# From the RWKV mixer to the mixture of experts, turned to token rows before the norm

## The chip, the cores and the metric

The kernel runs on one core of a Trainium2 chip. The metric is the device time of one launch in microseconds (us); a median over several runs is compared. The trace counts its times from the first instruction of the profiled execution.

## The reference

Two layers of a hybrid trunk on one sequence of 256 tokens of width 1024 (and 256 context tokens). Layer 0 is a Hyena mixer and a dense SwiGLU, layer 1 an RWKV-7 mixer and a mixture of eight experts. What matters here is the middle of layer 1:

```python
hx = layer_norm(ALPHA * hx + g1x * (y @ rw_w_out), ln_g[1, 0], ln_b[1, 0])
h = hx * (1.0 + sc2x) + sh2x
logits = h @ router                                # (256, 8)
top_val, top_idx = top_k(logits, 2)                # softmax over the two
fx = sum(combine[:, e] * ((silu(h @ w1[e]) * (h @ w3[e])) @ w2[e]) for e in range(8))
hx = layer_norm(ALPHA * hx + g2x * fx, ln_g[1, 1], ln_b[1, 1])
```

Everything is float32. An expert has 3 x 1024 x 3584 weights, and all eight are read in each launch.

## The kernel before

The program is written by hand, engine by engine, with semaphores. A tile called `arena` holds all of SBUF, and every stage lays its own names over it. In layer 1 the activations are kept channel-major: `XT[:, k, :]` holds channel tile k (of KT = 8, 128 channels each), with tokens along the row.

**RWKV.** Eight head pairs follow one another (`pair(i, more)`, L1464 on TensorE, L2276 on ScalarE, L2549 on POOL, L3038 on VectorE); the last has `more=False` and nothing ahead to prepare. Its gaps on TensorE are filled with the output product `YT @ rw_w_out`: `out_products` (L1455) takes the first seven of eight channel tiles of YT. The order of the eight output tiles is `OUT_ORDER`. `pair_done` (L3167) is raised by VectorE when YT is complete. Before that the SP queue has loaded each pair's weights (L861 to L892), and, once the last pair's gate product is done (L894), it loads the kept residual into XT, the router weights, the order table and the eight tiles `WO[k]` of rw_w_out, one after another (L896 to L903).

**The handover.** TensorE waits for `pair_done`, raises `expert_products` (L1686), and adds the last channel tile to the eight output sums (L1697). VectorE forms the residual of each tile (L3183), TensorE the mean (L1691), VectorE centres (L3190), ScalarE squares (L2371), TensorE forms the variance (L1704), ScalarE takes Ln and Exp (L2066, L2067), VectorE scales (L3196). ScalarE makes the modulated activation `UT` (L2379), and TensorE makes the logits as 8 rows (L1715), turns them and UT to token rows (L1719, L1725), and later XT scaled by POOL (L2593) for the residual y (L1732). The gate row of layer 1 is spread to all partitions by a product with a diagonal (POOL L2588, TensorE L1709, ScalarE L2376). ScalarE copies the turned rows to `UTOK` and `XTOK` (L2385, L2392).

**Choice and ranking, on VectorE.** Top two of eight (L3204 to L3216), a count of each token's place in its expert's list on TensorE (L1741 to L1745), the slot numbers (L3226, L3228), and `choose` (L3232), which makes the one-hot selection `pick` of the first expert; `first_expert` is raised. TensorE then gathers that expert's tokens (`gather`, L1751), and ScalarE and VectorE split the result in a high and a low part (L2397, L3237). Meanwhile VectorE ranks the experts by load (L3271 to L3289); POOL computes the combination shares (L2600 to L2605). `routed` counts these steps.

**Experts.** `large` and `small` alternate, four times: a large expert in 128 slots with split float32r products (`hidden_products` L1778, `down_products` L1809), a small one in 64 slots with plain float32 (L1863, L1897). Weights come through a ring of `ERN` = 8 slots of 1.5 to 2 MB, which ScalarE rounds to a high part (L2420) and VectorE to a low part (`low_digits`, L3247). On the SP queue each load (L919) waits for the step of `expert_products` that frees its slot; in the first round the slots that lie below `sq_at` are loaded at once, the others after `ln_scaled` 24 (L929). In the first large expert VectorE does a small yield (L3307), the first low digit, xg_low (L3237), three low digits, four additions to XTOK (L3301), then the up digits.

```python
for n, m in enumerate(OUT_ORDER):
    if n >= 4:
        mean3(n - 4)
    mm(out_sum(m), WO[KT - 1][:, m * P:(m + 1) * P], YT[:, KT - 1, :], start=False, stop=True,
       skip_group_check=True).then_inc(sem("out_full"), 1)
```

## Time and profile before

| | |
|---|---|
| median of 3 runs | 2230.41 us (2229.41 to 2232.9) |
| span of the profiled execution | 2236.2 us, 56085 instructions |
| granted TensorE clock over the span | 0.987 |
| TensorE busy | 2143.9 us (96%) |
| VectorE, ScalarE, POOL busy | 1177.1, 913.5, 179.7 us |
| DMA | 491.19 MB, mean 220 GB/s |
| last output tiles of the mixer to the first expert product | 1318.6 to 1354.6 us |

The profiled execution has no time of its own beside its span. Of the whole, the Hyena layer and its dense part take the first 780 us, RWKV the time to 1320, the experts the rest. A line of the profile names the engine and the line of the kernel (L1778), the operation, what it writes and reads, and a count; an entry "idle before <-" names what ended the idle time of the engine before it. PE is TensorE, PEld its weight load, DVE VectorE, ACT ScalarE, POOL GpSimd, and a q behind a name is an engine's instruction queue (SPq issues the DMAs).

### The profile page before, as it was taken

What the parts mean: (1) busy time and instruction counts of PE and PEld (TensorE: products, weight loads), DVE (VectorE), ACT (ScalarE), POOL (GpSimd) and SP (SyncE); (2) the same over time, 40 slices, a digit from 0 to 9 for tenths busy, and PEclk for the clock granted to TensorE, in tenths of its full rate; (3) what the DMA queues carried; (4) which work ended last, traced back from release to release, by engine and by line L of the source; (5) the groups of instructions that cost most, each with busy time, mean ns of one, the idle gap of its engine ahead of it and who ended that gap; (6) DMA issues with size and microseconds to landing.
All of it is one profiled execution on the core that took longest, in us unless ns stands there. A gap on an engine that the chain in (4) does not pass through costs nothing.

```text
span 2236.2 us, 56085 instructions
## 1 busy us (share of the span) xinstructions
PE 2143.9 (96%) x24686; PEld 1587.3 (71%) x24686; DVE 1177.1 (53%) x1581; ACT 913.5 (41%) x1196; POOL 179.7 (8%) x181
## 2 busy tenths in 40 slices
PE   8999999899999989999999899999999899989997
PEld 4577667688888747888888778953895399449843
DVE  3544595522233386666666539830982198129812
ACT  3422013522222185555555327720771177027600
POOL 2100272100000002200000100000000000000000
PEclk9999999999999999999999999999999999999999
DMA  8466406333322341111110258999999999999996
GB/s 292 153 225 235 160 1 184 118 94 94 95 94 101 99 153 35 35 35 35 35 35 26 80 202 317 366 363 407 406 407 398 407 407 407 403 406 407 407 405 259
DMA packets 220597, 491.19 MB, mean 220 GB/s; under 512 B 14631, under 2 KB 107711, under 8 KB 220095
## 3 DMA queue, kind: packets, MB, share of 16 engines
q1 hardware_dynamic: 218974, 482.44, 58.0%
q10 hardware_dynamic: 1442, 6.06, 0.8%
q8 instruction: 148, 2.42, 0.4%
q14 instruction: 33, 0.27, 0.0%
HBM read 486.37 MB, written 2.10 MB: 218 GB/s over the span
## 4 chain that ended last, share of the span: by engine, by line
PE 80%; DVE 5%; DMA 5%; SPq 4%; ACT 3%; issue 2%; POOL 0%; ACTq 0%; DVEq 0%
PE bank L1778 13%; PE bank L1809 7%; PE bank L1863 5%; SPq L919 4%; DMA expert_w<-in_moe_w_dram 4%; PE bank L1245 4%; PE bank L1246 4%; PE bank L1247 4%; PE bank L1151 2%; PE bank L1413 2%; PE bank L1122 2%; PE bank L1124 2%; PE bank L1123 2%; PE bank L1377 2%; PE bank L1262 2%
## 5 line engine op out<-in xcount | busy, mean ns | idle before, releaser
L3247 DVE TENSOR_TENSOR w_low<-expert_w,w_high 128x1792 fp32r<-128x1792 f32 (+1 forms) x192 | 383.8, 2023 | 43.2 <-ACT w_high L2420 41.5
L2420 ACT CAST w_high<-expert_w 128x1792 fp32r<-128x1792 f32 (+1 forms) x192 | 324.8, 1699 | 106.2 <-PE bank L1778 71.3
L1863 PE MATMUL bank<-expert_w,arena 128*64 128x448 f32 x1024 | 199.1, 541 | 1.5 <-DMA expert_w<-in_moe_w_dram 1.3
L1863 PEld LDWEIGHTS bank<-expert_w,arena 128*64 128x64 f32 x1024 | 72.3, 137 | 117.8 <-issue 116.7
L1778 PE MATMUL bank<-w_high,xg_high 128*128 128x448 f32 x512 | 147.0, 368 | 8.0 <-DVE xg_low L3237 7.7
L1778 PE MATMUL bank<-w_high,xg_low 128*128 128x448 f32 x512 | 145.1, 365 | 0.0
L1778 PE MATMUL bank<-w_low,xg_high 128*128 128x448 f32 x512 | 145.0, 364 | 0.0
L1245 PE MATMUL bank<-u_high,ring_high 128*128 128x512 f32 x352 | 138.7, 394 | 2.0 <-DVE u_low L2888 1.9
L1246 PE MATMUL bank<-u_low,ring_high 128*128 128x512 f32 x352 | 137.9, 392 | 0.0
L1247 PE MATMUL bank<-u_high,ring_low 128*128 128x512 f32 x352 | 137.6, 391 | 0.0
L2467 ACT ACTIVATE arena<-bank 128x448 f32<-128x448 f32 x16 | 8.7, 545 | 259.8 <-PE bank L1863 259.8
L1897 PE MATMUL bank<-expert_w,arena 128*64 128x512 f32 x448 | 101.6, 602 | 9.6 <-issue 8.9
L1778 PEld LDWEIGHTS bank<-w_high,xg_high 128*128 128x128 f32 x512 | 95.7, 190 | 19.2 <-DVE xg_low L3237 11.4
L1778 PEld LDWEIGHTS bank<-w_low,xg_high 128*128 128x128 f32 x512 | 97.0, 189 | 6.7
L1778 PEld LDWEIGHTS bank<-w_high,xg_low 128*128 128x128 f32 x512 | 96.8, 189 | 6.6
L3368 DVE TENSOR_TENSOR arena<-arena,bank 128x448 f32<-128x448 f32 x16 | 9.9, 621 | 158.1 <-PE bank L1863 158.1
L1809 PE MATMUL bank<-w_high,hid_high 128*128 128x512 f32 x224 | 88.0, 393 | 0.0
L1809 PE MATMUL bank<-w_high,hid_low 128*128 128x512 f32 x224 | 87.3, 390 | 0.0
L1809 PE MATMUL bank<-w_low,hid_high 128*128 128x512 f32 x224 | 87.2, 389 | 0.0
L1897 PEld LDWEIGHTS bank<-expert_w,arena 128*64 128x64 f32 x448 | 33.1, 138 | 72.5 <-issue 72.0
L2907 DVE TENSOR_TENSOR arena<-arena,bank 128x512 f32 (+1 forms) x22 | 15.1, 688 | 125.1 <-ACT arena L2157 125.1
L1245 PEld LDWEIGHTS bank<-u_high,ring_high 128*128 128x128 f32 x352 | 66.5, 189 | 16.9 <-issue 2.9
(454 smaller groups left out, 4208.6 us busy)
## 6 DMA issues: line engine op xcount, KB each, us to landing
expert_w<-in_moe_w_dram SPq DMA_DIRECT2D x128, 1792.0 KB, 18.6
expert_w<-in_moe_w_dram SPq DMA_DIRECT2D x32, 2048.0 KB, 19.3
arena<-in_mod_w_dram SPq DMA_DIRECT2D x48, 1024.0 KB, 8.6
expert_w<-in_moe_w_dram SPq DMA_DIRECT2D x32, 1536.0 KB, 18.9
arena<-in_ffn_w_dram SPq DMA_DIRECT2D x44, 512.0 KB, 5.0
arena<-in_hy_w_in_dram SPq DMA_DIRECT2D x12, 1024.0 KB, 5.3
arena<-in_rw_w_rkv_dram SPq DMA_DIRECT2D x48, 256.0 KB, 2.9
arena<-in_ffn_w_dram SPq DMA_DIRECT2D x11, 1024.0 KB, 4.8
```

The costliest lines, as they stand in the source:

```text
L919: sp.dma_start(dst, src).then_inc(expert_landed(s)[0], 16)
L1122: pe.matmul(bank[m % 4][:, :], wh[:, k, :], uh, start=(k == 0), stop=False)
L1123: pe.matmul(bank[m % 4][:, :], wh[:, k, :], ul, start=False, stop=False)
L1245: pe.matmul(bank[b + h][:, :], wh[:, c, :], uh, start=(k == 0), stop=False)
L1246: pe.matmul(bank[b + h][:, :], wh[:, c, :], ul, start=False, stop=False)
L1247: last = pe.matmul(bank[b + h][:, :], wl[:, c, :], uh, start=False, stop=(k == KT - 1))
L1778: last = pe.matmul(bank[b0 + v][:, 0:EH], x[:, k, :], w_[:, kk, v * EH:v * EH + EH], start=(k == 0 and x is XGH and w_ is wh), stop=(k == ...
L1809: last = pe.matmul(bank[4 + i_][:, :], x[:, f, :], w_[:, f - 4 * half, :], start=(c == 0 and f == 0 and x is HTH and w_ is wh), stop=(c == ...
L1863: last = pe.matmul(b[hd(v), 0:EH], small_x[:, k, :], w[:, kk, v * EH:v * EH + EH], start=(k == 0), stop=(k == KT - 1))
L1897: last = pe.matmul(bank[4][hd(v), :], small_hid[:, f, :], w[:, g, 512 * v:512 * v + 512], start=(c == 0 and f == 0), stop=(c == EC - 1 and ...
L2420: act.copy(high_piece(kind, n), piece(kind, ering[q % ERN], n // 2, n % 2))\
L3247: dve.tensor_tensor(piece(kind, low[s], n // 2, n % 2), piece(kind, ering[s], n // 2, n % 2), high_piece(kind, n).bitcast(F32), ALU.subtract)\
```

## The change

The handover is done by token. The residual tiles, now in `X3` (KT x 256), are turned to token rows directly behind the output product, in PSUM banks 0, 1, 4 and 5. VectorE takes mean and variance of each token by bn_stats, ScalarE one square root. The logits are made from the raw residual with router weights that hold the norm's gain and the modulation (`router_u`), and are corrected per token by the mean, the reciprocal deviation and two sums over the router's rows (`sum_row`). The normalised rows (`XTOK`) come from ScalarE, in four halves (`z_tok`). u is made of them with two rows of gain and shift, for tokens 0 to 127 on POOL, for tokens 128 to 255 on VectorE; y = ALPHA x (gain, shift) on POOL. The gain, shift and gate rows are stored to DRAM as three rows during pair 5's loads on SP and loaded again to all partitions. The loads of the residual and of the first four WO tiles follow the last pair's key product, and the router loads stand before the first pair. `expert_products` is raised before the last pair, the early slots are those below `x_at`, and the others wait for `out_full` 24. `OUT_ORDER` goes.

```diff
+        rows_kept = nc.dram_tensor("rows_kept", (3, D), F32, kind="Internal").ap()
...
-        low_k = 3
+        low_k = 4
+        WO = [arena[:, x_at + k * D:x_at + (k + 1) * D] for k in range(KT)]
+        u_gain, u_shift = (arena[:, x_at + 2 * KT * T + D * i:x_at + 2 * KT * T + D * i + D] for i in range(2))
...
-        early_slots = [s for s in range(ERN) if slot_at[s] + slot_words[s] <= sq_at]
+        early_slots = [s for s in range(ERN) if slot_at[s] + slot_words[s] <= x_at]
...
+            load("ld_router", rt_w, a["moe_router"][0].rearrange("(k p) e -> p k e", p=P))
+            load("ld_router", order_table, consts[4])
...
+                if i == KT - 3:
+                    sp.wait_ge(sem("rows_ready"), 1)
+                    for r, cols_ in enumerate((mod_g, mod_b, modv[1][:, 5 * KT:6 * KT, 0])):
+                        load("rows_kept", rows_kept[r].rearrange("(k p) -> p k", p=P), cols_)
...
-            step(sp, "ahead_products", "gate", KT - 1)
+            step(sp, "ahead_products", "keys", KT - 1)
             sp.wait_ge(sem("ld_tail"), 16)
             for k in range(0, KT, 2):
-                load("ld_tail", XT[:, k:k + 2, seg[1]], residual_kept[:, k:k + 2, :])
+                load("ld_tail", X3[:, k:k + 2, :], residual_kept[:, k:k + 2, :])
                 sp.wait_ge(sem("ld_tail"), 16 + 8 * (k + 2))
-            load("ld_tail", rt_w, a["moe_router"][0].rearrange("(k p) e -> p k e", p=P))
-            load("ld_tail", order_table, consts[4])
-            for k in range(KT):
-                load("ld_out", WO[k], a["rw_w_out"][k * P:(k + 1) * P, :])
-                sp.wait_ge(sem("ld_out"), 16 * (k + 1))
+            for name, row in (("ln_g", y_gain), ("ln_b", y_shift)):
+                load("ld_y_rows", row, a[name][1, 0:1, :].partition_broadcast(P))
+            sp.wait_ge(sem("rows_kept"), 48)
+            load("ld_row_gate", rowG, rows_kept[2:3, :].partition_broadcast(P))
+            for k in range(low_k):
+                load_wo(k)
+            step(sp, "ahead_products", "gate", KT - 1)
+            for k in range(low_k, KT):
+                load_wo(k)
+            for r, row in enumerate((u_gain, u_shift)):
+                load("ld_u_rows", row, rows_kept[r:r + 1, :].partition_broadcast(P))
             sp.wait_ge(sem("pair_done"), 2)
...
-                        sp.wait_ge(sem("ln_scaled"), 24)
+                        sp.wait_ge(sem("out_full"), 24)
...
+            pe.sem_inc(sem("expert_products"), len(STEPS["expert_products"]))
             pair(KT - 1, False)
+            pe.wait_ge(sem("rows_ready"), 1)
+            mm(bank[0][:, 0:2 * N_EXP], ones, router_sum, start=True, stop=True).then_inc(sem("sums_full"), 1)
             pe.wait_ge(sem("pair_done"), 2)
-            pe.sem_inc(sem("expert_products"), len(STEPS["expert_products"]))
             pe.wait_ge(sem("ld_out"), 16 * KT)
...
+            def turn_tile(m):
+                if m == 0:
+                    pe.wait_ge(sem("sums_taken"), 1)
+                pe.wait_ge(sem("residual_done"), 16 + m + 1)
+                for tt in range(2):
+                    last = pe.transpose(tok_bank(tt, m // 4)[:, m % 4 * P:m % 4 * P + P], X3[:, m, tt * P:tt * P + P], ident)
+                last.then_inc(sem("tile_turned"), 1)
+            def tile_logits(m):
+                for tt in range(2):
+                    last = mm(bank[2][:, tt * N_EXP:(tt + 1) * N_EXP], X3[:, m, tt * P:tt * P + P], router_u[:, m, :],
+                              start=(m == 0 and tt == 0), stop=(m == KT - 1), skip_group_check=True)
+                return last
+            for m in range(KT):
                 mm(out_sum(m), WO[KT - 1][:, m * P:(m + 1) * P], YT[:, KT - 1, :], start=False, stop=True,
                    skip_group_check=True).then_inc(sem("out_full"), 1)
+                if m >= 3:
+                    turn_tile(m - 3)
+            turn_tile(5)
+            tile_logits(0)
+            turn_tile(6)
+            tile_logits(1)
+            turn_tile(7)
+            for m in range(2, KT):
+                last = tile_logits(m)
             last.then_inc(sem("logits_full"), 1)
...
             pe.wait_ge(sem("first_expert"), 1)
+            pe.wait_ge(sem("u_tok"), 4)
             gather(0).then_inc(sem("first_expert"), 1)
...
+            act.activation(eps[:, 4:5], eps[:, 0:1], ACT.Sqrt)
+            act.wait_ge(sem("tok_var"), 1)
+            act.activation(stat[:, :, 2:3], whole[:, :, 1:2], ACT.Sqrt, bias=eps[:, 0:1]).then_inc(sem("tok_std"), 1)
+            for tt in range(2):
+                act.wait_ge(sem("tok_shift"), tt + 1)
+                for half in range(2):
+                    act.activation(XTOK[:, tt, half * 512:half * 512 + 512], tok_bank(tt, half)[:, :], ACT.Identity,
+                                   bias=stat[:, tt, 0:1], scale=stat[:, tt, 3:4]).then_inc(sem("z_tok"), 1)
+            act.wait_ge(sem("routed"), 2)
+            act.activation(w12[:, :, 1:2], w12[:, :, 0:1], ACT.Exp).then_inc(sem("w_exp"), 1)
+            act.wait_ge(sem("u_tok"), 4)
...
+                        act.wait_ge(sem("y_tok"), 2)
...
+            pool.wait_ge(sem("ld_y_rows"), 32)
+            for row in (y_gain, y_shift):
+                row_step(pool.tensor_scalar(row, row, float(ALPHA), 0.0, ALU.mult, ALU.add))
+            pool.wait_ge(sem("ld_u_rows"), 32)
+            for half in range(2):
+                cs = slice(half * 512, half * 512 + 512)
+                pool.wait_ge(sem("z_tok"), half + 1)
+                row_step(pool.tensor_tensor(UTOK[:, 0, cs], XTOK[:, 0, cs], u_gain[:, cs], ALU.mult))
+                pool.tensor_tensor(UTOK[:, 0, cs], UTOK[:, 0, cs], u_shift[:, cs], ALU.add).then_inc(sem("u_tok"), 1)
+            pool.wait_ge(sem("z_tok"), 4)
+            for tt in range(2):
+                row_step(pool.tensor_tensor(XTOK[:, tt, :], XTOK[:, tt, :], y_gain, ALU.mult))
+                pool.tensor_tensor(XTOK[:, tt, :], XTOK[:, tt, :], y_shift, ALU.add).then_inc(sem("y_tok"), 1)
...
             for i in range(KT - 1):
                 pair(i, True)
+                if i == 1:
+                    fold_router()
             pair(KT - 1, False)
...
+            for half in range(2):
+                dve.wait_ge(sem("tile_turned"), 4 * half + 4)
+                for tt in range(2):
+                    last = dve.bn_stats(out=halves[:, tt, 6 * half:6 * half + 6], in_=tok_bank(tt, half)[:, :])
+            link(last)
+            for tt in range(2):
+                last = dve.bn_aggr(out=whole[:, tt, :], in_=halves[:, tt, :])
+            last.then_inc(sem("tok_var"), 1)
...
+            dve.tensor_scalar(stat[:, :, 1:2], whole[:, :, 0:1], -1.0, None, ALU.mult)
+            centred_times_gain(0)
+            dve.wait_ge(sem("tok_std"), 1)
+            link(dve.reciprocal(stat[:, :, 3:4], stat[:, :, 2:3]))
+            dve.tensor_tensor(stat[:, :, 0:1], stat[:, :, 1:2], stat[:, :, 3:4], ALU.mult).then_inc(sem("tok_shift"), 1)
+            centred_times_gain(1).then_inc(sem("tok_shift"), 1)
...
             dve.wait_ge(sem("logits_full"), 1)
+            for tt in range(2):
+                last = dve.scalar_tensor_tensor(out=logit[:, tt, :], in0=sum_row[:, 0:N_EXP], scalar=stat[:, tt, 1:2],
+                                                in1=bank[2][:, tt * N_EXP:(tt + 1) * N_EXP], op0=ALU.mult, op1=ALU.add)
+            link(last)
+            for tt in range(2):
+                last = dve.scalar_tensor_tensor(out=logit[:, tt, :], in0=logit[:, tt, :], scalar=stat[:, tt, 3:4],
+                                                in1=sum_row[:, N_EXP:2 * N_EXP], op0=ALU.mult, op1=ALU.add)
...
             dve.sem_inc(sem("routed"), 1)
+            scaled_plus_shift(0)
             dve.wait_ge(sem("places_full"), 1)
...
             choose(0, slot_no).then_inc(sem("first_expert"), 1)
+            scaled_plus_shift(1)
+            dve.tensor_tensor(w12[:, :, 0:1], mx[:, :, 1:2], mx[:, :, 0:1], ALU.subtract).then_inc(sem("routed"), 1)
...
+            dve.wait_ge(sem("w_exp"), 1)
+            link(dve.tensor_scalar(w12[:, :, 0:1], w12[:, :, 1:2], 1.0, None, ALU.add))
+            link(dve.reciprocal(w12[:, :, 2:3], w12[:, :, 0:1]))
+            link(dve.tensor_tensor(w12[:, :, 3:4], w12[:, :, 2:3], w12[:, :, 1:2], ALU.mult))
...
+                        dve.wait_ge(sem("y_tok"), 2)
                         added((6, 7, 2, 3))
```

`centred_times_gain` takes the mean from a turned half in PSUM and multiplies by u_gain, `scaled_plus_shift` multiplies by the reciprocal deviation and adds u_shift, both for tokens 128 to 255. `fold_router` makes mod_g, mod_b, router_u and router_sum in seven small instructions.

## Rows read from the trace of the kernel before

**Rows 1.** Stretches: length, busy by engine, POOL last; granted clock, DMA share, GB/s.

```profile
1320.00:1350.00 30.00, 25.61 (x139) 18.22 (x137) 14.76 (x53) 17.11 (x29) 6.32 (x13) 0.94 1.03 407
1350.00:1360.00 10.00, 7.40 (x35) 5.86 (x36) 9.92 (x8) 7.59 (x7) 0.34 (x3) 1.00 0.29 115
1360.00:1480.00 120.00, 119.82 (x607) 106.44 (x607) 100.69 (x70) 81.59 (x64) 0.00 (x0) 1.00 0.95 352
1490.00:2190.00 700.00, 680.02 (x3488) 456.71 (x3486) 351.92 (x268) 297.69 (x294) 0.00 (x0) 0.99 1.03 405
```

**Rows 2.** SP queue's waits, 1240 to 1620 us: total, times, longest.

```profile
SPq L929 <- DVE arena L3196: 7.0, 1, 7.0
SPq L919 <- PEq L1686: 6.2, 1, 6.2
```

**Rows 3.** TensorE's timeline, 1318 to 1355 us: start, length, engine, line.

```profile
1318.58 0.59 PE L1697 MATMUL bank<-arena 128*128 128x256 f32 x2
...
1345.84 3.81 PE L1751 MATMUL bank<-arena 128*128 128x128 f32 x32 [0.23 <-DVE arena L3232]
...
1354.59 0.67 PE L1778 MATMUL bank<-w_high,xg_high 128*128 128x448 f32 x2 [1.37 <-DVE xg_low L3237]
```

**Rows 4.** VectorE's timeline, 1323 to 1364 us.

```profile
1323.96 0.48 DVE L3183 SCALAR_TENSOR_TENSOR arena<-bank,arena 128x256 f32<-128x256 f32 x1 [0.38 <-PE bank L1697]
...
1341.42 0.17 DVE L3202 COPY arena<-bank 128x16 f32<-128x16 f32 x1 [0.83 <-PE bank L1725]
...
1345.21 0.48 DVE L3232 TENSOR_SCALAR arena<-arena 128x128 f32<-128x128 f32 x2
...
1348.61 0.17 DVE L3289 TENSOR_TENSOR arena<-arena 128x16 f32<-128x16 f32 x1
...
1353.17 1.29 DVE L3237 TENSOR_TENSOR xg_low<-bank,xg_high 128x512 fp32r<-128x512 f32 x2
...
1362.57 2.02 DVE L3247 TENSOR_TENSOR w_low<-expert_w,w_high 128x1792 fp32r<-128x1792 f32 x1
```

**Rows 5.** Lines L3385 and L3391 (min/median/max ns), and ScalarE's timeline at 1343 us.

```profile
L3385 DVE BATCH_NORM_STATS2 arena<-bank x4: 681/687/698, 2224.1 to 2229.2; 128x6 f32<-128x512 f32 x4
...
L3391 DVE SCALAR_TENSOR_TENSOR arena<-bank,arena x4: 743/747/752, 2225.7 to 2230.8; 128x512 f32<-128x512 f32 x4
...
1343.74 1.07 ACT L2392 ACTIVATE arena<-bank 128x512 f32<-128x512 f32 x2
```

**Rows 6.** POOL's and VectorE's timelines around 891, 69, 286 and 1278 us, and line L2678.

```profile
890.82 0.68 DVE L2992 TENSOR_TENSOR arena<-arena 128x512 f32<-128x512 f32 x1
...
891.59 1.27 POOL L2532 TENSOR_TENSOR arena<-arena 128x512 f32<-128x512 f32 x1 [14.05 <-DVE arena L2992]
892.82 1.71 POOL L2532 TENSOR_TENSOR arena<-arena 128x512 f32<-128x512 f32 x1
...
892.14 1.27 DVE L2996 TENSOR_TENSOR arena<-arena 128x512 f32<-128x512 f32 x1
...
69.76 1.25 POOL L2495 TENSOR_TENSOR arena<-arena 128x512 f32<-128x512 f32 x1
...
L2678 DVE TENSOR_SCALAR arena<-arena x3: 174/174/649, 70.4 to 254.0; 128x16 f32<-128x16 f32 x3
...
286.75 1.75 DVE L2842 TENSOR_TENSOR arena<-arena 128x512 f32<-128x512 f32 x1
...
1278.76 1.90 POOL L2588 TENSOR_TENSOR arena<-arena 128x1024 f32<-128x1024 f32 x1
```

**Rows 7.** Two microseconds between two experts, columns as in rows 1.

```profile
1568.00:1570.00 2.00, 1.29 (x4) 0.01 (x1) 1.97 (x2) 2.00 (x3) 0.00 (x0) 0.56 1.04 406
```

**Rows 8.** Key weights of pair 6: SP's issue, ScalarE's first use; VectorE behind pair 1.

```profile
1096.15 3.20 SPq L871 DMA_DIRECT2D arena<-in_rw_w_rkv_dram  x2
...
1128.45 1.05 ACT L2218 CAST keys_w_high<-arena 128x1024 fp32r<-128x1024 f32 x1
...
966.57 0.45 DVE L3046 COPY_PREDICATED arena<-arena,bank 128x256 f32<-128x256 int32 x1 [1.92 <-PE bank L1472]
```

183 lines of the change are left out of this document (57 added, 126 removed).

## Prediction

> **What bounds the kernel now.** I read the stretches of time first. From 1490 to 2190 us the DMA queues move 405 GB/s: the expert weights set the pace there. At the handover they do not: they run full from 1320 to 1350, fall to 115 GB/s in the next ten microseconds and come to 352 in the first large expert, to 1480, in which TensorE is busy 119.82 of 120 us [rows 1]. The ring of eight slots is full, and a load starts when TensorE frees a slot. So what the change is worth is read at one place: how much earlier TensorE gets through the first large expert. Every later load follows from those slots, and the tail moves by the same amount.
>
> The SP queue's waits come second: 6.2 us for PE's queue at L1686, past the pair's end, and 7.0 us for the scaled tiles of L3196 [rows 2]. Then TensorE's timeline: the last output tiles start at 1318.58, the gather for the first expert at 1345.84 and its first gate product at 1354.59 [rows 3]. Between them stands a chain of norm, router, ranking and choice. Its last part runs on VectorE: the choice ends at 1345.69, the ranking at 1348.78, and then come the small yield, a low digit and xg_low, which ends at 1354.46 [rows 4]. VectorE is still the late one in the first gate: its first up digit ends at 1364.59, when TensorE is ready for it [rows 4]. Hence the measure is VectorE's chain: **each microsecond by which xg_low moves is a microsecond of the kernel**, up to the 23 us of queue that are unused there (10 x 292/407 and 120 x 55/407).
>
> **What goes and comes before the choice.** The output tiles still end about 1320.5, one small product (sums) later, at most 0.4 us by a tile of L1697 [rows 3]. Eight residuals of 0.48 us follow as before and end at 1324.2 [rows 4]; the transposes ride between the tiles, so the last ends near 1325.4. New on VectorE: four bn_stats of 0.69 (two before that moment, two after), two aggregations, the first product of 0.75, reciprocal and shift 0.4, the second 0.75 [rows 5], small ones at 0.2: 1329.1. ScalarE's root falls beside the first product, and its table is loaded long before. The router products left behind the last transpose are 24 instructions, at the gather's rate (32 in 3.81 [rows 3]) 2.9: 1328.3, hidden. Two pairs of logit instructions, 0.4 each as the small ones of rows 4 have it, and then from the copied logits to the choice 3.6 (3.79 less the copy) and 0.48 as now [rows 4]: the choice would be made at **1334.0** instead of 1345.7, 11.7 earlier. What it takes out is the mean, variance, Ln, Exp, eight scalings, the 8-row logits and half of 32 transposes.
>
> **What comes behind the choice.** One shifted product (0.7) and the weights' four small steps (0.7) now stand in the chain: 1.4 back. Unhindered, xg_low would come 10.3 to 10.5 us earlier.
>
> **Who shares the way.** The change puts eight POOL instructions exactly there: four of 128x512 for u from the first z half (1329.0: the shift at 1328.4 and one ScalarE half of 0.54 [rows 5]) and four of 128x1024 for y. POOL's multiply of 128x512 takes 1.27 us alone; 128x1024 took 1.90 once, with broadcast inputs, and twice 1.27 is 2.54 [rows 6]. I take 2.4, nearer to the same kind. So POOL is busy from 1329.0 to 1334.4 with u and to about 1344.7 with y.
> And such an instruction holds VectorE up. One of two SBUF inputs, 128x512, took 1.27 instead of 0.68 when it began 0.55 into POOL's: it ended 0.6 after POOL's end, and the next POOL instruction then took 1.71. A tensor_scalar of 16 elements took 649 ns against 174, until POOL's end; and when two VectorE instructions stood back to back, POOL went between them and the second took 1.75 [rows 6]. The two take turns, whole instructions at a time.
> The Trainium skill says so too (SBUF — State Buffer, Who interferes with whom): a VectorE instruction with two SBUF inputs contends with a GpSimd instruction that reads SBUF, the port pair is locked for a whole instruction, and tensor_scalar can fall under it as well. By that rule the sum is the one below, against this change; by a mere slowing of both it would be near the 10.4. The trace agrees with the lock [rows 6].
>
> **The sum under turns.** Before the choice VectorE has nine instructions of this kind: the second logit pair, two is_equal, two for the chosen, one shifted product, two for the pick. POOL has eight. Each waits for about one POOL instruction, so the choice comes when POOL ends, 1344.7 and not 1334.0. After it VectorE is free: 0.7 for the second half of u, 3.1 for the ranking (1345.69 to 1348.78 [rows 4]), 0.7 for the weights: 1349.2 against 1348.78, **0.4 us later**. If the short tensor_scalars did not wait, five stand before the choice, the four y instructions catch the second half, the subtraction, "above" and "moves", and the chain ends 1.2 earlier. With y at 1.90 all is 2.0 earlier, with 2.54 0.6 later. I take 0.4 us of gain, between the two readings; this case's own range is 3.2 of gain to 3.0 of loss (0.4, 0.6 and 2 for a slow gather, see next). The gather then starts at 1345.5 as now and needs 3.8 [rows 3]. The granted clock fell to 0.56, towards its 1.2 GHz level, after a pause of TensorE between experts [rows 7]; as it now pauses before the gather, that may take 2 to 4 us more, of which the yield and the low digit on VectorE cover 2. The wait for y before the four additions comes to nothing: VectorE gets there at 1360, 15 us behind POOL's end. Nor does that of ScalarE's first Silu.
>
> **What costs nothing.** Loads from the pair's end: SP gets over L1686's wait, so the first load goes out 6.2 us earlier, and the later slots wait for out_full. Worth nothing: the ring is full some 6 us sooner and waits the longer. Were TensorE ever quicker by more than the 23 us, it would count. SP gets past no reader of the X3 loads, row broadcasts and w_out loads: they are issued in the seventh pair instead of after it, one behind another, and their readers (POOL's scaling, the last pair's products) stay where they are; after the gate step only four w_out loads and the two u rows are left of twelve, so these too land before today's last one. The three scattered stores of 4 KB stand before pair 6's key weights: they were issued at 1096.15, needed at 1128.45 [rows 8], a cover of 28 us. Row stores of this kind are not in the trace; the nearest are two key half-loads, 3.20 [rows 8], 1.6 each; from above I put 9 us each, the cover divided by three, and take 3. Beyond 9 pair 6 would start late. fold_router, seven small instructions of 0.2 as in rows 4, 1.4 us, stands at the end of pair 1, where VectorE waits 1.92 us for the scores [rows 8]. POOL's two row scalings take the place of the diagonal (1.90 [rows 6]) with VectorE idle.
>
> **Rivals.** (1) *No turns for such short work*: VectorE goes on beside POOL. For: three of its instructions here read PSUM, which is free of it. Against: rows 6. Gain 10.4, less 1.7 should the clock be at half (0.5) for the first 3.5 us of products: 2220.0 to 2221.7. (2) *The queue is the bound all along*, so its start counts: 6.2 us gained, 2224.2. Against: 115 GB/s while TensorE is full [rows 1]. (3) *Slower*: POOL's four y instructions, in place on a tile ScalarE has just written, need more than 2.4. VectorE's pick waits for the last: each microsecond on one is four on the kernel. From 3.5 us on (4 x 1.1) it is slower by 0.2%; at 4.0, 2236.4. Against: 1.90 and 2.54. (4) *The change doesn't do what it says*: the loads don't start at the pair's end, as another semaphore holds SP. No time hangs on it: 2230.0 as forecast.
>
> **Numbers.** The profiled execution spans 2236.2 us, 5.8 over the median of 2230.41; the page shows nothing around the span. The sum makes 2235.8 of it, and I carry the difference over to the median: 2230.0. Chances: turns 0.70 (with (4) in it), rival (1) 0.17, rival (2) 0.05, rival (3) 0.08. A measurement of this kernel tells 0.2%, 4.5 us, from no change. Faster by more: 0.17, 0.05 and 0.03 of the first case, 0.25; slower: 0.08 and 0.01; the rest same. The range reaches into (1) and (2) below and into the start of (3) above: 2221 to 2234; the likeliest case's own is 2227.2 to 2233.4.
>
> **What would show it.** POOL with eight tensor instructions from 1329 to about 1345; VectorE's is_equal, chosen and pick at 1 to 2.5 us instead of 0.2; the gather near 1345; first gate product near 1354.5; DMA idle for over ten microseconds before 1360; first load 6 us earlier than now. Wrong, if the pick is done by 1335 while POOL still works, or if the first gate product starts before 1350.

## The result and the profile after

The changed kernel takes **2248.59 us** (median of 4 runs, 2245.00 to 2252.93) against 2230.08 for the kernel before on the same chip: a ratio of 1.0096, 95% interval 1.0083 to 1.0109. It is 18.5 us slower, where 2230.0 was forecast and the range ended at 2234.

The stretches of the changed kernel's profile, at the times that answer to [rows 1]:

```profile
core 0: us, PE busy (x) PEld busy (x) DVE busy (x) ACT busy (x) POOL busy (x), PEclk, DMA share, GB/s
1320.00:1350.00 30.00, 20.25 (x119) 18.32 (x117) 19.06 (x39) 4.37 (x6) 10.63 (x7) 0.82 1.02 394
1350.00:1360.00 10.00, 4.73 (x23) 4.76 (x24) 8.86 (x24) 3.17 (x3) 5.20 (x7) 0.52 0.73 287
1360.00:1370.00 10.00, 8.55 (x46) 6.81 (x45) 9.92 (x8) 7.81 (x7) 0.47 (x3) 1.00 0.01 2
1490.00:2190.00 700.00, 679.08 (x3476) 456.46 (x3474) 354.31 (x271) 298.53 (x295) 0.00 (x0) 1.00 1.03 405
```

The expert stage is as it was: 405 GB/s. The queues are now full from 1320 on, and they stand still (2 GB/s) before TensorE frees the first slot. So I cut the span at marks that both kernels have: the first scores product of a pair, the first of the last output tiles (L1697 before, L1734 after), the end of the first expert's choice, its first gate product, and the transposes of its first hidden tile, behind gate and up. All in us, each from one profiled execution; "before again" is a second profile of the kernel before.

| | first pair at | 5th to 6th pair | 7th to 8th | first to last pair | last pair to out tiles | choice | first gate | first turned tile | end |
|---|---|---|---|---|---|---|---|---|---|
| before | 849.8 | 56.76 | 56.47 | 398.5 | 70.3 | 27.1 | 36.0 | 65.4 | 917.6 |
| before again | 846.8 | 56.46 | 56.79 | 398.7 | 70.0 | 25.7 | 34.6 | 64.0 | 913.0 |
| changed | 842.4 | **72.16** | **60.16** | 417.4 | 69.4 | 25.4 | 35.5 | 64.9 | 914.5 |

The last four columns count from the last output tiles' start. The handover, the aim of the change and the subject of the forecast, is where it was. The loss lies before it: **18.9 us between the first and the last pair**, 15.4 in one step and 3.7 in another. The starts differ from run to run (the first modulation loads took 37.5 us in the profile of before and 31.7 in that of the changed kernel), so I compare the columns and leave the start out.

TensorE's timeline in the fifth pair shows the loss, in the two products of the level loop (L1440, L1451; L1413, L1424 before):

```profile
start us, us, engine line op out<-in xcount [idle before <-releaser]
1087.42 1.40 PE L1451 MATMUL bank<-arena 32*32 32x32 f32 x128
1089.14 1.31 PE L1440 MATMUL bank<-arena 32*32 32x32 f32 x106 [0.32 <-DVE arena L3053]
1090.66 0.48 PE L1440 MATMUL bank<-arena 32*32 32x32 f32 x3 [0.20 <-issue]
1092.33 0.35 PE L1440 MATMUL bank<-arena 32*32 32x32 f32 x4 [1.19 <-issue]
...
1094.86 0.59 PE L1440 MATMUL bank<-arena 32*32 32x32 f32 x5 [0.92 <-issue]
...
1098.45 1.31 PE L1451 MATMUL bank<-arena 32*32 32x32 f32 x19 [1.15 <-issue]
1100.97 0.26 PE L1451 MATMUL bank<-arena 32*32 32x32 f32 x2 [1.20 <-issue]
...
1103.87 1.32 PE L1451 MATMUL bank<-arena 32*32 32x32 f32 x61 [0.17 <-issue]
1105.12 1.97 PE L1336 MATMUL bank<-arena 128*128 128x128 f32 x8
```

A batch of 128 takes 1.4 us as a rule. Here the two batches of the level loop's fourth and last round take 16 us, and all but the first 106 products come in crumbs of 1 to 61. The gaps are put down to "issue": no wait for another engine or for data is seen. The same two stretches in both kernels, the round and the five batches behind it (changed kernel first each time), give the loss in two parts:

```profile
1089.14:1105.12 15.98, 8.30 (x256) 0.63 0.56 17
1096.63:1099.38 2.75, 2.75 (x257) 1.00 0.34 95
1105.12:1111.42 6.30, 6.30 (x104) 0.57 0.16 45
1099.38:1103.34 3.96, 3.96 (x103) 1.00 0.24 70
```

(Columns: us, TensorE busy and products, granted clock, DMA share, GB/s.) The gaps and the slow crumbs cost 13.2 us. The granted clock fell to 0.50, the 1.2 GHz level, at 1093.44, after TensorE had begun to stand still, and stayed there for 17.07 us; so the batches behind, which have no gaps, took another 2.3 us more. The SP queue says what had just been issued:

```profile
1087.71 1.63 SPq L772 DMA_DIRECT2D rows_kept<-arena  x3
1089.39 18.49 SPq L883 DMA_DIRECT2D arena<-in_rw_w_rkv_dram  x2
```

L772 with `rows_kept` are the three stores of 4 KB, L883 is the key weights behind them. And the queues' view of 24 us, first the changed kernel, 1083 to 1107 us:

```profile
DMA packets 4368, 0.62 MB, mean 26 GB/s; under 512 B 3184, under 2 KB 4368, under 8 KB 4368
q1 hardware_dynamic: 4368, 0.62, 43.8%
```

then the kernel before in the same part of its fifth pair, 1090.5 to 1114.5:

```profile
DMA packets 1808, 0.96 MB, mean 40 GB/s; under 512 B 85, under 2 KB 1803, under 8 KB 1803
q1 hardware_dynamic: 1803, 0.88, 12.7%
q8 instruction: 5, 0.08, 1.3%
```

The three stores are 12 KB in 3072 packets of 4 bytes. Queue q1 holds the 16 engines for 43.8% of the stretch, but not by these: read packet by packet, those under 512 bytes took 32.5 us of engine time, 8.5%. Four times as much, 135.8 us, went to packets of 512 bytes, 117.1 of it to the 512 of them that started behind the stores: single ones took up to 3.7 us, where none took over 0.25 in the kernel before.

Queue q8, which fetches instructions 16 KB at a time (0.08 MB by 5), has no packet in these 24 us, and five in the kernel before. It is tempting to read this as the cause: TensorE runs some 90 tiny products per microsecond here (128 in 1.4 us), and its next instructions are late. But the packets do not come by time, they come by the place in the code, the same in each pair. The level loop has four rounds of 256 products; one packet starts as the first round ends, and the next only behind the loop, in pairs 4 to 7 of both kernels. From the one to the other, in the kernel before and in the changed kernel:

```profile
1090.56:1101.71 11.15, 10.47 (x793) 1.00 0.27 78
1082.30:1107.88 25.58, 16.89 (x814) 0.72 0.41 25
```

About as many products pass between the two packets, in 11.15 and in 25.58 us. So no packet is missing in the changed kernel; it comes late because TensorE was late. The stalled round had run its code three times already. **That the stores hold TensorE up is tested below; by which way is not shown**: a late fetch through q8 is not what this view shows.

The Trainium skill (Advanced Engine Details and Errata, ISA Cache) says that an instruction cache line is 16 KB or 256 instructions: the packets' size agrees. The Trainium skill also says (DMA: Bandwidth & Descriptors, Rules for kernel authors) that a non-contiguous last dimension becomes one descriptor per element and should be rearranged: the 3072 packets agree.

The handover after, on VectorE, against [rows 4]:

```profile
1338.98 0.21 DVE L3231 SCALAR_TENSOR_TENSOR arena<-arena,bank 128x8 f32<-128x8 f32 x1
1339.23 1.33 DVE L3235 SCALAR_TENSOR_TENSOR arena<-arena 128x8 f32<-128x8 f32 x2
1341.80 1.32 DVE L3246 TENSOR_SCALAR arena<-arena 128x8 f32<-128x8 f32 x2
1343.15 3.47 DVE L3249 SCALAR_TENSOR_TENSOR arena<-arena 128x8 f32<-128x8 f32 x2
1346.77 2.81 DVE L3217 SCALAR_TENSOR_TENSOR arena<-arena 128x512 f32<-128x512 f32 x1
1349.69 2.11 DVE L3257 TENSOR_SCALAR arena<-arena 128x2 f32<-128x2 f32 x1
1351.83 2.63 DVE L3261 TENSOR_SCALAR arena<-arena 128x128 f32<-128x128 f32 x2
1363.21 1.29 DVE L3266 TENSOR_TENSOR xg_low<-bank,xg_high 128x512 fp32r<-128x512 f32 x2
```

and on POOL, for which [rows 6] gave the price:

```profile
1339.13 1.26 POOL L2588 TENSOR_TENSOR arena<-arena 128x512 f32<-128x512 f32 x1 [46.92 <-ACT arena L2378]
...
1344.26 2.34 POOL L2592 TENSOR_TENSOR arena<-arena 128x1024 f32<-128x1024 f32 x1
1348.98 2.79 POOL L2592 TENSOR_TENSOR arena<-arena 128x1024 f32<-128x1024 f32 x1
1351.85 2.34 POOL L2593 TENSOR_TENSOR arena<-arena 128x1024 f32<-128x1024 f32 x1
```

The pair of logit steps that reads a bank takes 0.21 each. Among the steps with SBUF inputs alone eight took longer than they do alone, one for each of POOL's eight instructions, and each ends within 0.6 us after one of them. A tensor_scalar of two columns takes 2.11 us.

### The profile page after: what moved, and what is told of

The parts are those of the page before. It is cut to its first block, busy times and chain, and to the rows that moved or that the text cites. A ratio compares the mean times of both kernels' runs of the same rounds, so it can differ in the third digit from the quotient of the medians.

```text
span 2243.6 us, 56018 instructions
## 1 busy us (share of the span) xinstructions
PE 2133.4 (95%) x24650; PEld 1585.4 (71%) x24650; DVE 1190.1 (53%) x1593; ACT 905.1 (40%) x1177; POOL 190.2 (8%) x182
## 3 DMA queue, kind: packets, MB, share of 16 engines
HBM read 488.99 MB, written 2.11 MB: 219 GB/s over the span
## 4 chain that ended last, share of the span: by engine, by line
PE 79%; DVE 6%; DMA 5%; SPq 4%; ACT 3%; issue 3%; POOL 1%; ACTq 0%; DVEq 0%
PE bank L1786 13%; PE bank L1817 7%; PE bank L1868 5%; SPq L946 4%; DMA expert_w<-in_moe_w_dram 4%; PE bank L1272 4%; PE bank L1273 4%; PE bank L1274 4%; PE bank L1440 2%; PE bank L1178 2%; PE bank L1149 2%; PE bank L1451 2%; PE bank L1151 2%; PE bank L1150 2%; PE bank L1404 2%
## 5 line engine op out<-in xcount | busy, mean ns | idle before, releaser
L1902 PEld LDWEIGHTS bank<-expert_w,arena 128*64 128x64 f32 x448 | 32.5, 137 | 69.7 <-issue 69.2
L1149 PE MATMUL bank<-u_in_high,proj_high 128*128 128x512 f32 x192 | 78.4, 408 | 0.0
## 6 DMA issues: line engine op xcount, KB each, us to landing
expert_w<-in_moe_w_dram SPq DMA_DIRECT2D x32, 1536.0 KB, 18.9
```

Source lines behind the costliest of these rows:

```text
L1149: pe.matmul(bank[m % 4][:, :], wh[:, k, :], uh, start=(k == 0), stop=False)
L1902: last = pe.matmul(bank[4][hd(v), :], small_hid[:, f, :], w[:, g, 512 * v:512 * v + 512], start=(c == 0 and f == 0), stop=(c == EC - 1 and ...
```

## The experiments

Theory **S**: the 4-byte stores hold up TensorE's instruction stream (the expectations also say how, by instructions that arrive late; that part stays unproven, as said). Theory **L**: VectorE and POOL take turns at memory, so the handover gains nothing. Rivals are named with each run. "The kernel before" below is the one timed on the same chip with the runs.

**Fewer pieces (e1_runs32).** The same bytes, with the eight words of a partition side by side in DRAM. The rows come back permuted, so this one computes other values.

```diff
-load("rows_kept", rows_kept[r].rearrange("(k p) -> p k", p=P), cols_)
+load("rows_kept", rows_kept[r].rearrange("(p k) -> p k", k=KT), cols_)
```

> The changed kernel with the same three stores of 4 KB, but each partition's eight numbers side by side in DRAM (128 runs of 32 bytes in place of 1024 runs of 4 bytes, so 384 pieces in place of 3072). The rows come back in another order than the reference's. Theory S (the 4-byte pieces hold the DMA engines and TensorE's own instructions arrive late): the step from the fifth pair to the sixth, 72.16 us in the changed kernel, returns to about 56.5 to 58 us; the time falls by 14 to 15.5 us, to about 2230 where the start is the quick one of 2245, and 2237 where it is the slow one of 2252. Rival K (a wait of the pair on the key weights or on the row data, whatever the size of the pieces): the step stays at 70 us or more. Rival F (VectorE's added fold or the rest of the change): also stays.

Measured: the step is 58.51 us instead of 72.16, first to last pair 401.1 instead of 417.4. The time is 2235.62 us (6 runs, 2231.43 to 2240.58) against 2229.34, ratio 1.0035 (1.0019 to 1.0050): 13 us below the changed kernel, not quite the 14 to 15.5. K and F fall: bytes and waits are as in the changed kernel, and the loss is gone but for 2.0 us.

It is not the 384 pieces of the expectation, though. Two of the rows went out in 32-byte runs. The gate row, every second word of its tile in SBUF, still went word by word, now to neighbouring addresses. The DMA view of 1091.5 to 1094.5 us has 1328 small packets:

```profile
DMA packets 1330, 0.01 MB, mean 5 GB/s; under 512 B 1328, under 2 KB 1330, under 8 KB 1330
```

Of these 256 are the runs of 32 bytes and 1024 the gate row's words, so 1280 pieces in all, and most of the latter ran just behind the level loop instead of in it. So this run says that the form of the stores makes the loss; how much is their number, their places in DRAM or their moment, it does not say.

**One store in each of three pairs (e2_one_each).**

```diff
-if i == KT - 3:
+if 3 <= i <= 5:
     sp.wait_ge(sem("rows_ready"), 1)
-    for r, cols_ in enumerate((mod_g, mod_b, modv[1][:, 5 * KT:6 * KT, 0])):
+    r, cols_ = i - 3, (mod_g, mod_b, modv[1][:, 5 * KT:6 * KT, 0])[i - 3]
```

> The changed kernel with one of the three scattered stores in each of three pairs' loads (numbers 3, 4 and 5) in place of three in number 5. Theory S with a cost in proportion to the pieces: three steps of about 56.5 + 5 = 61.5 us, the same total. Theory S with a buffer of instructions ahead that covers a short hole (the three stores took 15.4 us off the step while their pieces were in flight about 18 us, so some 3 us were covered once): each store then costs 5.8 - 3 = about 2 to 3 us, and the time falls by 6 to 9 us. Rival K (late key weights): each store alone lies well within the cover of 28 us and costs nothing, the time falls by 15 us.

Measured: the three steps become 64.53, 64.47 and 66.29 us, 8 to 10 each, and the time 2259.10 us, *longer* than with the three together. All three readings missed; nearest was S with a cost in proportion, at 61.5, and furthest K. TensorE in the first of these pairs:

```profile
977.86 1.10 PE L1440 MATMUL bank<-arena 32*32 32x32 f32 x83 [0.32 <-DVE arena L3053]
980.80 0.54 PE L1440 MATMUL bank<-arena 32*32 32x32 f32 x7 [1.84 <-issue]
```

The store had been issued at 976.08. Even a single one in this loop costs about 8 us, and each further one right behind it some 4 ((15.4 - 8) / 2). In the third of these pairs it is the gate row that is stored: 1024 pieces of 4 bytes, 512 bytes apart in DRAM, cost 9.8 us in the loop, where e1's 1024 of the same row, side by side and behind the loop, cost 2.0 together with the rest.

**The stores alone, in the kernel before (e4_before_stores, e7_stores_in_ffn).** Three such stores of values nobody reads, once in the sixth pair's loads, once between the loads of the dense layer.

```diff
     sp.wait_ge(sem("ld_pair"), landed + LD_PAIR)
+    if i == KT - 3:
+        for r in range(3):
+            load("rows_kept", rows_kept[r].rearrange("(k p) -> p k", p=P), modv[1][:, (3 + r) * KT:(4 + r) * KT, 0])
```

> The kernel before with nothing but three scattered stores of 4 KB put into the loads of the sixth pair, from columns of the modulation that are ready since the start (values nobody reads). Theory S: the step from the fifth pair to the sixth grows from 56.76 to about 72 us and the time by 14 to 16 us, to about 2245. Rival K or F (the loss comes from what else the change moved): the time stays at 2230, within 2 us.

Measured: the step is 72.34 us, the time 2244.27 against 2229.34, ratio 1.0075 (1.0047 to 1.0103). The stores do it alone, and K and F fall here too.

> The kernel before with three scattered stores of 4 KB (from modulation columns ready long before, values nobody reads) in the dense layer, between the loads of w13 and of w2, near 600 us, where TensorE's products have 128 to 512 columns and take 0.1 to 0.4 us each, and where a load has some ten microseconds to spare. Theory S (it is the instructions that are late, about 90 of them per microsecond in a pair and under 10 here): the time grows by less than 3 us. Rival W (any work slows while 4-byte pieces hold the DMA engines): it grows by 8 to 15 us as in the pair.

Measured: 2229.02 us against 2228.82, ratio 1.0003 (0.9993 to 1.0013). TensorE stays full while the pieces are in flight (issued at 583.99, landed after 13.4 us), as its stretch and the queues' view of 582 to 600 us say:

```profile
582.00:600.00 18.00, 18.00 (x81) 1.00 0.49 65
```

```profile
DMA packets 5226, 1.17 MB, mean 65 GB/s; under 512 B 3152, under 2 KB 5200, under 8 KB 5226
rows_kept<-arena SPq DMA_DIRECT2D x3, 4.0 KB, 13.4
```

81 products in 18 us, 4.5 per microsecond against 90 in a pair. The same stores cost 15 us in one place and nothing in the other, and W falls. That what counts is how many instructions per microsecond TensorE needs is the reading that fits, and it is argued: the two places differ in their loads too. Both are loops of the program, and both stretches are without a q8 packet.

**The rows turned on the chip first (e5_turned).** The three columns of eight are put side by side, one VectorE transpose of 32x32 blocks turns them, and four stores of 24 runs of 128 bytes write the rows.

```diff
+for r, v in enumerate((mod_g, mod_b, modv[1][:, 5 * KT:6 * KT, 0], mod_g)):
+    last = dve.tensor_copy(rows_in[:, r * KT:(r + 1) * KT], v)
+link(last)
+dve.transpose(rows_turned, rows_in).then_inc(sem("rows_ready"), 1)
...
+for b in range(4):
+    load("rows_kept", rows_kept.rearrange("r (k b i) -> b (r k) i", b=4, i=32)[b], rows_turned[32 * b:32 * b + 24, :])
```

> The changed kernel, with the three rows put together as 32 columns, turned by one VectorE transpose of 32x32 blocks, and stored by four transfers of 24 runs of 128 bytes: 96 pieces in place of 3072, the values as in the changed kernel. Theory S: the step from the fifth pair to the sixth is 56.5 to 57.5 us (58.51 with 384 pieces), and the time from the first pair's scores to the end of the span, 1401.2 us in the changed kernel and 1386.4 in the one before, becomes 1384 to 1386. Rival P (the 3.7 us more of the step of the seventh pair come from the output weights and the rows being loaded there, not from the stores): that step stays at 60 us, and the time from the first pair's scores to the end is 1387 to 1389. If the 3.7 us hang on the stores too, it is 56.5 to 57.5.

Measured: the step is 56.50 us, first pair to end 1385.4, and the time **2229.79 us against 2228.82, ratio 1.0008 (0.9995 to 1.0021)**: with 96 pieces the change is what was forecast of it, no difference. The seventh pair's step is 57.66, between the two guesses. Over the eleven kernels of this study that have the residual, row and output weight loads in the seventh pair, it is 56.44 to 63.72 us, 59.0 in the mean; over the four profiles that load them a pair later, 56.44 to 56.79, and the last pair is hardly longer for it there (69.7 against 69.6). The gaps are "issue" again, beside loads of 512 KB; the worst one, in the kernel e11 below:

```profile
1223.61 0.29 PE L1633 MATMUL bank<-arena 64*64 64x64 f32 x4
1227.67 1.01 PE L1633 MATMUL bank<-arena 64*64 64x64 f32 x26 [3.77 <-issue]
```

So **this move costs 2.3 us in the mean** (59.0 less 56.6, and 0.1 back) and up to 7, with one profile of each kernel. Here the instruction queue does show something. This is code outside any loop, and q8's packet starts at 1225.32, within the gap; TensorE goes on 1.4 us after it has landed. In undisturbed pairs this packet starts 68 to 82 products before this point. The gaps of 2.6 us in the changed kernel and in e9 look the same (packet in the gap, TensorE back 1.3 to 1.4 us after the landing). So in these three a late instruction fetch is seen; that the big loads delay it was not tried by itself. In e11 the clock fell to its lower level behind the gap too, for 10.24 us.

**The kernel before again (e0_before_again).**

> The kernel before, unchanged, for a second profile of it. Its profiled execution spanned 2236.2 us, while its other runs are at 2224 to 2233. If only the start of the program differs from run to run (the first modulation loads took 37.5 us here and 31.7 us in the changed kernel's profile), the time from the first pair's scores to the end is 1386 us again, within 1 us, and the first pair's scores start at 843 or 850 us. If the part behind differs too, it is 1380 to 1385 or so, and the comparison has to allow for it.

Measured: 1381.7 us from the first pair to the end, so the part behind differs by some 5 us from run to run: 1.4 in the choice and most of the rest in the expert stage. Columns of one profile are compared to within that; the pairs' steps (56.4 to 56.9) are much steadier.

**y behind the choice (e3_y_late), y behind the shares (e6_turned_y_last).** The first on the changed kernel, the second with the turned rows.

```diff
 pool.wait_ge(sem("z_tok"), 4)
+pool.wait_ge(sem("first_expert"), 1)
 for tt in range(2):
     row_step(pool.tensor_tensor(XTOK[:, tt, :], XTOK[:, tt, :], y_gain, ALU.mult))
```

> The changed kernel with GpSimd's four 128x1024 instructions for y put behind the choice of the first expert (a wait on first_expert), so that they no longer lie beside VectorE's routing. Theory L (VectorE and GpSimd take turns at memory, and these four hold up the small steps of the routing): from the start of the last output tiles to the first gate product 35.5 us become 27 to 31 us and the time falls by 5 to 8 us against the changed kernel; the step of the fifth pair stays at 72 us. Rival D (the expert weights' transfers or the clock bound the handover): the first gate product stays within 1 us of where it is, and the time too. Rival T (the turns are only moved: y now holds up the gathered digits): the choice comes 5 to 9 us earlier but the first gate product gains under 3.

Measured: the choice ends at 18.7 us instead of 25.4, but the first gate product comes at 37.4 instead of 35.5, and the time stays (2249.74 us). Rival T was right; the first gate product even lost 1.9 us: four steps of the ranking now took 2.0 to 2.7 us each in place of 0.2 to 0.6. The step of the fifth pair is 69.91 us here: the stores were issued later in the pair, and their gaps lie behind the level loop, in code outside any loop. There a packet of q8 did take 4.3 us, where 0.9 to 1.5 is usual, so in such code a late fetch may have its part. So the three stores cost 13.3 to 15.7 us in the three profiles that have them in this pair, and not in the loop alone.

> As the kernel with the turned rows, and GpSimd's four 128x1024 instructions for y stand behind the combination shares, so behind VectorE's ranking too. Theory L (turns): the choice ends about 19 us after the last output tiles' start (25.4 in the changed kernel, 18.7 where y began right behind the choice), the ranking and GpSimd's shares are done at about 24, y runs to about 34 and takes turns with VectorE's low digits of the weights; the first gate product starts 27 to 30 us after the last output tiles' start in place of 35.5, and 2 to 3 us are given back in the gate's low digits: 3 to 6 us less than with the turned rows alone. Rival T (the turns cost the same wherever y stands): within 1.5 us of the kernel with the turned rows. Rival D (the expert weights bound the start): the gate products start earlier, but the end does not move.

Measured: first gate product at 30.4 us, 5.1 earlier, yet the first turned tile at 65.1 instead of 64.9, and 2233.09 us, no gain (ratio to the kernel before 1.0020, 1.0008 to 1.0033). The timelines of VectorE and POOL in the gate, then TensorE's waits in the first expert (sum, times, longest):

```profile
1336.69 3.57 DVE L3280 TENSOR_TENSOR w_low<-expert_w,w_high 128x1792 fp32r<-128x1792 f32 x1
1341.50 11.17 DVE L3280 TENSOR_TENSOR w_low<-expert_w,w_high 128x1792 fp32r<-128x1792 f32 x3
```

```profile
1346.71 4.07 POOL L2604 TENSOR_TENSOR arena<-arena 128x1024 f32<-128x1024 f32 x1
```

```profile
PE bank L1788 <- DVE w_low L3280: 3.6, 3, 1.6
PE bank L1788 <- DVE xg_low L3270: 2.9, 1, 2.9
```

A low digit takes 3.6 to 3.7 us instead of 2.0, POOL's instruction 4.1 instead of 2.3. Wherever y stands between the last tiles and the up products, VectorE pays for it.

**y left out, u left out (e8_no_y, e9_no_y_no_u).** With the turned rows; POOL's instructions are cut to 8 columns, so y, and in the second also half of u, is not computed.

```diff
-row_step(pool.tensor_tensor(XTOK[:, tt, :], XTOK[:, tt, :], y_gain, ALU.mult))
+row_step(pool.tensor_tensor(XTOK[:, tt, 0:8], XTOK[:, tt, 0:8], y_gain[:, 0:8], ALU.mult))
```

> The kernel with the turned rows, and GpSimd's four instructions for y cut from 1024 to 8 columns each, so that the residual y is left out but for 8 columns; u stays. Theory L (turns): the choice ends 18.7 us after the last output tiles' start as where y stood behind it, the ranking behind it is free too, and the first gate product starts at 28 to 29.5 us in place of 35.5; nothing is given back in the gate, so the first expert's first turned hidden tile, at 64.9 us, comes at 58 to 59, and from the last output tiles' start to the end 914.2 us become 907 to 909. Rival D (past the gate's start the weights' transfers set the pace): the gate starts early, but the distance to the end stays at 913 to 915.

> As the kernel with y cut to 8 columns, and GpSimd's four 128x512 instructions for the first half of u cut to 8 columns too, so that u is left out there. Theory L: VectorE is alone, the choice ends at 15 to 15.5 us after the last output tiles' start, 10 less than in the changed kernel, as was worked out for the way without turns; the first gate product starts at 25 to 27 us, with the gather at TensorE's lower clock, and the distance to the end becomes 904 to 907. If u's four instructions cost nothing (rival: only the long ones matter), it is that of the kernel without y.

| | choice | first gate | first turned tile | end | time | kernel before |
|---|---|---|---|---|---|---|
| turned rows | 25.4 | 35.5 | 64.9 | 914.2 | 2229.79 | 2228.82 |
| no y | 18.7 | 28.9 | 58.3 | 909.0 | 2223.65 | 2227.00 |
| no y, half of u | 15.5 | 25.7 | 55.1 | 905.9 | 2222.15 | 2227.00 |

The ratios to the kernel before are 0.9984 (0.9969 to 0.9999) and 0.9969 (0.9957 to 0.9981). L holds to the numbers: without POOL the choice comes 9.9 us earlier, near the 10.3 to 10.5 worked out for the way without turns. 9.8 us at the first turned tile are 8.3 at the end. D falls.

**The loads put back (e10_loads_late).**

```diff
-pe.sem_inc(sem("expert_products"), len(STEPS["expert_products"]))
 pair(KT - 1, False)
...
 pe.wait_ge(sem("pair_done"), 2)
+pe.sem_inc(sem("expert_products"), len(STEPS["expert_products"]))
```

> The kernel with the turned rows, with the start of the expert loads put back behind the last pair, where the kernel before has it. My forecast was that the early start is worth nothing, as the ring only fills sooner: the first load goes out some 6 us later, the idle time of the queues before the first slot comes free is shorter by as much, and the distance from the last output tiles to the end stays at 914.2 within 1.5 us. Rival Q (the queue's start counts): it grows by 5 to 6 us.

Measured: 64.9 and 914.7 us, 2230.04 against 2227.00, ratio 1.0011 (0.9995 to 1.0026), as with the turned rows and early loads (1.0008). The start is worth nothing that shows.

**Two of y's four instructions moved to the end (e11_shift_at_end, e12_shift_by_pool).** With y behind the shares. The added row goes on at the very end: by TensorE in the first, by POOL during the last down products in the second.

```diff
+pe.matmul(bank[2 * tt + half][:, :], ones[0:1, :], last_shift[0:1, half * 512:half * 512 + 512], start=False, stop=False)
```

> The kernel with the turned rows and with y behind the shares, where GpSimd does only the two multiplications of y; the additive row of y is loaded as one row at the end and added by four small products of TensorE with a row of ones, ahead of the last sum. Theory L: two long instructions less take half of the turns out of the gate: the first gate product starts at 30.4 us as with y last, TensorE waits there for the low digits 1 to 2 us in place of 3.6, the first turned hidden tile comes at 62.5 to 63.5 us (64.9, 65.1), and the time is 1.5 to 2.5 us less than with the turned rows alone, 2227 to 2228.5, just below the kernel before. If what is given back does not come from the turns, it stays at 65 us.

Measured: first turned tile at 60.9 us, 4.0 earlier, end at 913.9; 2229.25 us (ratio 1.0002, 0.9986 to 1.0018). The four row products stand in the last chain; two of them:

```profile
2215.50 1.12 PE L1939 MATMUL bank<-arena 1*128 1x512 f32 x2
...
2217.61 1.12 PE L1939 MATMUL bank<-arena 1*128 1x512 f32 x2
```

```diff
+pool.wait_ge(sem("ld_y_rows"), 32)
+row_step(pool.tensor_scalar(last_shift, last_shift, float(ALPHA), 0.0, ALU.mult, ALU.add))
+for tt in range(2):
+    pool.tensor_tensor(XTOK[:, tt, :], XTOK[:, tt, :], last_shift, ALU.add).then_inc(sem("y_tok"), 1)
```

> The kernel with the turned rows, y behind the shares with GpSimd's two multiplications only, and the additive row of y loaded to all partitions behind the last expert's weights, scaled and added to the residual rows by GpSimd (one 128x1024 scaling and two 128x1024 additions, about 7 us), while TensorE is in the last expert's down products; no products of TensorE for it. The kernel with the row added by TensorE won 4.0 us at the first turned hidden tile (60.9 against 64.9 us) and gave 3 to 4 back at the end, where its four extra pairs of products took 4 x 1.1 us ahead of the last sums. Theory L with E (the rest was given back by those products alone): 60.9 again, and from the last output tiles to the end 910 to 911 us in place of 914.2; the time 2224 to 2227, some 1 to 3 us less than the kernel before. Rival G (a microsecond won at the first expert is lost to the weights' queue before the end anyway): 913 to 915 us and no less time than before.

Measured: **2225.54 us against 2228.33, ratio 0.9992 (0.9982 to 1.0002)**, the lowest median of the kernels that compute everything, but not told apart from the kernel before. In its profile the first turned tile stands at 62.2, the end at 913.9: 2.7 us won and 2.4 lost again in the expert stage, which differs by as much between two profiles of one kernel. Between E and G this stays open.

## Why the prediction was wrong

**Where it failed: "What costs nothing", the three scattered stores.** They were priced at 3 us of the SP queue each, bounded at 9, behind a cover of 28 us for pair 6's key weights, and so put into the sum at nothing. They cost 15.4 us of a pair (13.3 to 15.7 over three kernels). Two errors stand in that step. The size was taken from two key half-loads [rows 8], whose pieces are 512 bytes long: 512 of them, where a store of 4 KB has 1024. And the bound asked only *who waits for what stands behind on the SP queue*. The key weights were indeed not late; the sentence "Beyond 9 pair 6 would start late" named the wrong victim. What was late is TensorE's own issue: 13.2 us in the last round of the level loop, and 2.3 us behind it, as its clock had fallen by then. That the stores do this is shown (e4, e5, e2). By which way they reach TensorE stays open: no instruction packet is missing in the loop, and no other way was tried (whether the trace's own records of so many instructions come into it, for one).

**Also in that step: the loads moved into the seventh pair**, priced at nothing as no reader waits. They cost 2.3 us in the mean, 3.7 in the profile shown; in its longest gap, 2.6 us, an instruction fetch is late.

**What was right.** The rest of the forecast stands: with the scattered stores out of the way, e5_turned gives 1.0008 (0.9995 to 1.0021). That number also holds the 2.3 us of the seventh pair, which no term of the forecast has.
- *Turns.* The choice was forecast 26.1 us behind the last output tiles (1344.7 less 1318.6) and came at 25.4; the gain at the first gate product 0.4 us and was 0.5 (36.0 to 35.5), but the four profiles with the old handover have 34.6 to 36.0 there, so a gain this small is not told from none. Eight steps waited, one for each POOL instruction, as the sum has it; only six of them are among its nine. e8 and e9 show that POOL's two groups hold it: 6.7 us for y, 3.2 for half of u.
- *POOL's y at 2.4 us*: 2.34, 2.35, 2.79, 2.34. Rival (3), the only slower one, did not happen; the kernel is slower for a reason that was no rival.
- *One misreading* without effect: by [rows 4] the eight residuals end at 1324.4 (1323.96 and 0.48), not 1324.2.
- *Rival (1)* is what happens without POOL: 9.9 us at the choice.
- *The gather at the low clock*: 5.91 us instead of 3.81 at a granted clock of 0.52 in that stretch, the 1.2 GHz level, after TensorE had stood idle for 6.24 us. As said, VectorE's yield and low digit covered it.
- *Loads from the pair's end*: the first at 1318.99, 10.1 us before the last tiles instead of 3.8, worth nothing that shows (e10); so rival (2) falls.

**Half right: the measure.** "Each microsecond by which xg_low moves is a microsecond of the kernel" holds only if VectorE is free afterwards. In e6 the gate began 5.1 us sooner and was through at the same time, since the low digits took turns. The first turned tile is the mark that carries to the end (9.8 us there, 8.3 at the end).

## What to carry to other kernels

Count a transfer's pieces before its bytes, and ask of every burst of small pieces what TensorE does while it is in flight: the loss came where it ran 90 products per microsecond, in gaps that no queue's view names, and the clock fell behind them. A column that must become a row is turned on the chip first; or it is stored beside long products, where it cost nothing here. Before an absent packet is called a late one, count the work between the packets in a run that is not disturbed. And work for POOL beside a chain of short VectorE steps is not hidden by being on another engine; moving it later helps only if VectorE is idle there.

## What was not expected of the hardware

- Three stores of 1024 pieces of 4 bytes held TensorE up for 13.2 us in a loop of tiny products, though the data queue moved only 26 GB/s in that time; the two 256 KB loads behind them took SP 18.5 us to issue, 3.3 otherwise, and single packets of 512 bytes took up to 3.7 us.
- The clock then stood at its lower level for 17.07 us, worth another 2.3.
- Cost in a pair's step: three stores with 3072 pieces of 4 bytes 13.3 to 15.7 us, one with 1024 8 to 10, and 96 pieces of 128 bytes none that shows. 1024 pieces of 4 bytes side by side with 256 of 32, mostly behind the loop, 2.0.
- The same 3072 pieces beside products of 0.2 us cost nothing (ratio 1.0003, 0.9993 to 1.0013).
- The instruction queue has no packet for the last three rounds of a loop of 256 products, about 770 products, in any profile looked at.
- When a long VectorE instruction (128x1792, 2.0 us) and a long POOL one (128x1024, 2.3 us) take turns, each is longer by nearly the other's rest: 3.7 and 4.1 us.
